# Tokens loaded ahead of the weights in the first modulation, and the last expert's rows added by a product

## The reference, cut to what matters

```python
# the first thing computed: the modulation of layer 0, from the vectors c and c_ctx
m_lat = adaln(c, w_mod[0], b_mod[0])          # silu(c) @ w_mod[0] + b_mod[0]; 1024 x 9216 weights
m_ctx = adaln(c_ctx[None], w_mod[0], b_mod[0])
# the last thing computed: each token goes to its two best experts of one group
yb  = (silu(xb @ w_gate[e]) * (xb @ w_up[e])) @ w_down[e]     # xb: up to 128 tokens of expert e
out = x + gate_1 * y_of_first_choice + gate_2 * y_of_second_choice
```

## Time and profile before

| | us |
|---|---|
| median of three executions | 3731.35 |
| lowest, highest | 3731.34, 3735.18 |
| the profiled execution's own time | 3733.24 |
| its span in the profile | 3731.5 |

### The profile page before, as it was taken

How to read it: one execution, slowest core, us unless ns; L and a number is a source line. 1 busy time by engine, 2 the same in 40 slices (tenths; PEclk the granted TensorE clock), 3 DMA queues, 4 the chain that set the end, 5 groups by cost and what they waited for, 6 DMA issues and landing times. The chain is left out here.

```text
span 3731.5 us, 44636 instructions
## 1 busy us (share of the span) xinstructions
PE 3499.3 (94%) x17456; PEld 2872.2 (77%) x17456; DVE 2191.0 (59%) x2933; ACT 1510.1 (40%) x1696; POOL 437.9 (12%) x321
## 2 busy tenths in 40 slices
PE   7999999888999999999989999798998998999996
PEld 5888888655888888888658888777876866888885
DVE  6635446548744466557886333552235337999996
ACT  4112111547422242223445222434444235777774
POOL 2000000200110011001112000200000012334441
PEclk9999999899999999999999999999998998999998
DMA  6333323210334325444112322131222326999996
GB/s 241 116 99 102 112 89 101 65 57 1 100 127 146 119 86 191 151 155 145 58 44 68 102 91 90 52 129 57 84 85 74 96 88 245 356 354 354 361 367 240
DMA packets 315224, 522.35 MB, mean 140 GB/s; under 512 B 18500, under 2 KB 274545, under 8 KB 289200
## 3 DMA queue, kind: packets, MB, share of 16 engines
q1 hardware_dynamic: 304016, 507.06, 39.5%
q0 software_dynamic: 11040, 12.91, 1.0%
HBM read 519.91 MB, written 25.17 MB: 146 GB/s over the span
## 5 line engine op out<-in xcount | busy, mean ns | idle before, releaser
L536 PE MATMUL banks<-operand_hi,trunk_weights_hi 128*128 128x512 f32 (+1 forms) x1568 | 568.4, 363 | 36.0 <-DVE operand_lo L1093 10.9
L536 PE MATMUL banks<-operand_lo,trunk_weights_hi 128*128 128x512 f32 (+1 forms) x1568 | 559.3, 357 | 0.0
L536 PE MATMUL banks<-operand_hi,trunk_weights_lo 128*128 128x512 f32 (+1 forms) x1568 | 559.2, 357 | 0.0
L536 PEld LDWEIGHTS banks<-operand_hi,trunk_weights_hi 128*128 128x128 f32 x1568 | 300.1, 191 | 84.0 <-issue 33.4
L536 PEld LDWEIGHTS banks<-operand_lo,trunk_weights_hi 128*128 128x128 f32 x1568 | 300.4, 192 | 41.3 <-issue 0.5
L536 PEld LDWEIGHTS banks<-operand_hi,trunk_weights_lo 128*128 128x128 f32 x1568 | 299.9, 191 | 41.5
L4172 DVE TENSOR_TENSOR ex_w_lo<-weight_ring,ex_w_hi 128x2048 fp32r<-128x2048 f32 x128 | 288.9, 2291 | 41.7 <-ACT ex_w_hi L4107 41.7
L1320 DVE TENSOR_TENSOR trunk_weights_lo<-weight_ring,trunk_weights_hi 128x2048 fp32r<-128x2048 f32 x90 | 206.6, 2296 | 177.1 <-ACT trunk_weights_hi L1275 177.1
L1275 ACT ACTIVATE trunk_weights_hi<-weight_ring 128x2048 fp32r<-128x2048 f32 x90 | 171.7, 1908 | 216.8 <-PE banks L536 216.3
L4107 ACT ACTIVATE ex_w_hi<-weight_ring 128x2048 fp32r<-128x2048 f32 x128 | 241.8, 1914 | 22.4 <-PE banks L4022 22.4
L536 PE MATMUL banks<-trunk_hidden_hi,trunk_weights_hi 128*128 128x512 f32 (+1 forms) x672 | 233.4, 347 | 4.4 <-DVE X L1822 1.9
(11 more groups left out here) (597 smaller groups left out, 7381.4 us busy)
## 6 DMA issues: line engine op xcount, KB each, us to landing
weight_ring<-ffn_w SPq DMA_DIRECT2D x120, 1024.0 KB, 5.2
weight_ring<-w_mod SPq DMA_DIRECT2D x72, 1024.0 KB, 5.1
weight_ring<-w_gate SPq DMA_DIRECT2D x64, 1024.0 KB, 6.1
weight_ring<-w_up SPq DMA_DIRECT2D x64, 1024.0 KB, 7.2
room<-w_down SPq DMA_DIRECT2D x64, 1024.0 KB, 7.2
weight_ring<-w_in SPq DMA_DIRECT2D x26, 1024.0 KB, 5.2
weight_ring<-ffn_w SPq DMA_DIRECT2D x16, 768.0 KB, 4.8
weight_ring<-o_w_pw SPq DMA_DIRECT2D x8, 1024.0 KB, 5.4
```

Source lines behind the costliest of these rows:

```text
L536: ins = pe.matmul(bank[:, at:at + width], w, x[:, at:at + width], start=start and n == 0, stop=stop and n == len(passes) - 1)
```

## The change

Opening:

- The tokens are the first large loads, as three of 1 MB with a semaphore each. Chunks 0 to 3 follow without a wait.
- All 48 transposes and 12 copies come before the first product, through the half banks 4, 5 and 7 instead of 0, 1, 2, 3 and 7.
- Each chunk is split and multiplied in two halves of 1024 columns, each with its own semaphore step: `w_hi`, `w_lo`, and four matmuls.
- The reload of a slot waits for the second half of its chunk.

End of the kernel:

- Routing also computes `last_gates`, the gate of each token towards the last slot column that runs, zero where it isn't there: four VectorE instructions.
- GpSimd, after the first two gathers, clears half of `YS`, copies the last slot column's ids, fills `hot` with 0 to 511, and scatters the zeros to the rows of the last column. It waits for these zeros before the second expert's scatter.
- The last expert's result is no longer scattered. ScalarE alone copies it to `YS`. VectorE makes `hot`, which is 1 where slot and token meet, and eight f32 matmuls of 512 columns multiply it with `YS`.
- The block `combine` is gone. In the experts' own block SP waits for the last weights' split and for GpSimd's word that all other scatters have landed, loads the chosen rows into the ring's four slots and stores the results. VectorE adds the chosen rows for all four tiles, then the product with `last_gates`, in eight halves of 512 columns.

```diff
@@ opening, SP
-            W.issue(sp, SLOTS)
-            W.used[0] = lambda i, r: (s_lo, r + 1)
-            W.issue(sp, SLOTS + 2)
-            sp.dma_start(rows[:, 0:ST, :], a["x"][0].rearrange("(t p) d -> p t d", p=P)).then_inc(s_x, 16)
-            sp.dma_start(rows[:, ST:, :], a["ctx"][0].rearrange("(t p) d -> p t d", p=P)).then_inc(s_x, 16)
-            W.ahead(sp, lambda i, r: (s_lo, r + 1))
+            for i, src in enumerate((a["x"][0][0:2 * P], a["x"][0][2 * P:], a["ctx"][0])):
+                sp.dma_start(rows[:, 2 * i:2 * i + 2, :], src.rearrange("(t p) d -> p t d", p=P)).then_inc(s_x[i], 16)
+            W.ahead(sp, lambda i, r: (s_lo, 2 * r + 2))
@@ opening, TensorE
+                for piece in range(2):
+                    pe.wait_ge(s_lo, 2 * n + piece + 1)
+                    for part, w in enumerate((w_hi, w_lo)):
+                        for q in range(2 * piece, 2 * piece + 2):
...
+            for j in range(2 * NT):
+                turn_tokens(j)
             pe.wait_ge(s_clo, 1)
@@ opening, ScalarE (VectorE alike, with its subtraction)
-                if n >= 2:
-                    act.wait_ge(s_done, n - 1)
-                act.activation(w_hi[:, n % 2, :], raw, ACT.Copy).then_inc(s_hi, 1)
+                for at in (0, 1024):
+                    if n >= 2:
+                        act.wait_ge(s_done, 2 * n - 3 + at // 1024)
+                    act.activation(w_hi[:, n % 2, at:at + 1024], raw[:, at:at + 1024], ACT.Copy).then_inc(s_hi, 1)
@@ routing, VectorE
+            link(dve.tensor_scalar(in_last[:], blk[:], cmax[:], -1.0, ALU.subtract, ALU.is_equal))
+            link(dve.tensor_tensor(in_last[:], in_last[:], hot[:, :, :, EXPERTS - 1].rearrange("p c t -> p (c t)"), ALU.mult))
+            link(dve.tensor_tensor(in_last[:], in_last[:], gates[:].rearrange("p c t -> p (c t)"), ALU.mult))
+            link(dve.tensor_tensor(last_gates[:], in_last[:, 0:ST], in_last[:, ST:], ALU.add))
@@ experts, SP
+            sp.wait_ge(s_lo, nth(n, 1, UP[1]))
+            sp.wait_ge(s_landed, 1)
+            for t in range(ST):
+                sp.dma_start(taken(t), chosen[:, :, t, :]).then_inc(s_y[t], 16)
+            for t in range(ST):
+                sp.wait_ge(s_sum, 2 * t + 2)
+                sp.dma_start(rows[:, t, :], XR[:, t, :]).then_inc(s_store, 16)
+            sp.wait_ge(s_store, 16 * ST)
@@ experts, GpSimd
             gather(0, 1)
+            pool.memset(YS[:, 1, :], 0.0).then_inc(s_clear, 1)
+            pool.tensor_copy(id_now[1][:], ids[:, span(n * 2 + 1, 1)]).then_inc(s_clear, 1)
+            pool.iota(hot, pattern=[[1, S]], base=0, channel_multiplier=0, allow_small_or_imprecise_dtypes=True).then_inc(s_lane, 1)
+            pool.wait_ge(s_clear, 2)
+            pool.indirect_dma_start(out=k.expert_out, out_offset=bass.IndirectOffsetOnAxis(ap=id_now[1][:, 0:1], axis=0),
+                                    in_=YS[:, 1, :], in_offset=None, bounds_check=2 * S - 1, oob_is_err=False).then_inc(s_zero, 16)
...
             scatter(n, 0)
-            scatter(n, 1)
-            for u in range(2):
-                pool.wait_ge(s_ys[u], n * 16 + 16)
+            pool.wait_ge(s_ys[0], n * 16 + 16)
+            pool.wait_ge(s_ys[1], n * 16)
+            pool.sem_inc(s_landed, 1)
@@ experts, TensorE
+            pe.wait_ge(s_hot, 1)
+            for t in range(ST):
+                for half in range(2):
...
+                    pe.matmul(OWN(t)[:, at], hot[:, t * P:(t + 1) * P], YS[:, 1, at], start=True, stop=True).then_inc(s_own, 1)
@@ experts, VectorE
-            rows_out(n, 2)
...
+            dve.tensor_scalar(hot, hot, token_last[:], None, ALU.is_equal).then_inc(s_hot, 1)
...
+                    dve.scalar_tensor_tensor(XR[:, t, :], taken(t)[:, c, :], gates[:, c, t:t + 1], XR[:, t, :], ALU.mult, ALU.add).then_inc(done, 1)
+            for t in range(ST):
+                dve.wait_ge(s_2, t + 1)
+                for half in range(2):
...
+                    dve.scalar_tensor_tensor(XR[:, t, at], OWN(t)[:, at], last_gates[:, t:t + 1], XR[:, t, at], ALU.mult, ALU.add).then_inc(s_sum, 1)
```

More of the change, by code:

```diff
@@ L356, in load_and_modulate @@
         sem = lambda n: k.sem(f"ld_{n}")
-        s_con, s_first, s_vec, s_x, s_zero, s_clear, s_vt, s_vc, s_silu, s_chi, s_clo = (
-            sem("consts"), sem("first_vectors"), sem("vectors"), sem("tokens"), sem("vector_zeros"), sem("cleared"), sem("vectors_turned"),
+        s_x = [sem(f"tokens{i}") for i in range(NT // 2)]
+        s_con, s_first, s_vec, s_zero, s_clear, s_vt, s_vc, s_silu, s_chi, s_clo = (
+            sem("consts"), sem("first_vectors"), sem("vectors"), sem("vector_zeros"), sem("cleared"), sem("vectors_turned"),
             sem("vectors_copied"), sem("silu"), sem("cond_hi"), sem("cond_lo"))
@@ L420, in product @@
             def product(n):
[L421 to L427, removed]
+                for piece in range(2):
+                    pe.wait_ge(s_lo, 2 * n + piece + 1)
+                    for part, w in enumerate((w_hi, w_lo)):
+                        for q in range(2 * piece, 2 * piece + 2):
+                            kk, r = (n, q) if n < KD else (2 * (n - KD) + q // 2, 4 + q % 2)
+                            ins = pe.matmul(half(r), cond4[:, kk, :], w[:, n % 2, 512 * q:512 * q + 512],
+                                            start=kk == 0 and part == 0, stop=kk == KD - 1 and part == 1)
+                    ins.then_inc(s_done, 1)
             pe.wait_ge(s_con, 16)
@@ L509, in _ @@
                 if c == KD:
[L510 removed]
+                    dve.wait_ge(s_done, 2 * KD)
                     for r in (1, 3):
@@ L3632, in mixture @@
         k.raw_landed = [k.sem(f"ex_raw_landed{c}") for c in range(CHUNKS)]
-        project_and_route(k, MX, XR, XG, gates, pairs, ids, tokens)
-        experts(k, XR, XG, pairs, ids, tokens)
-        combine(k, XR, gates, out)
+        project_and_route(k, MX, XR, XG, gates, last_gates, pairs, ids, tokens)
+        experts(k, XR, XG, pairs, ids, tokens, gates, last_gates, out)
 CHUNKS = 6
@@ L3931, in _, with experts @@
                 pool.tensor_tensor(squares[:, 0, :], squares[:, 0, :], squares[:, m, :], ALU.add).then_inc(s_sum, 1)
-def experts(k, XR, XG, pairs, ids, tokens):
+def experts(k, XR, XG, pairs, ids, tokens, gates, last_gates, out):
     nc = k.nc
@@ L3953, in experts @@
         s_free = [sem(f"rows_free{i}") for i in range(2)]
+        s_y = [sem(f"chosen{t}") for t in range(ST)]
+        s_landed = sem("rows_landed")
+        s_clear, s_zero, s_lane, s_token, s_hot, s_1, s_2, s_own, s_sum, s_store = (
+            sem("rows_cleared"), sem("zeros_scattered"), sem("lanes"), sem("last_token"), sem("last_hot"), sem("first_choice"),
+            sem("second_choice"), sem("last_rows"), sem("sums"), sem("stored"))
+        token_last = sb("token_last", [P, 1])
+        hot = k.x_sum[:, 0:S]
+        chosen = k.expert_out.rearrange("(c t p) d -> p c t d", c=2, p=P)
+        taken = lambda t: k.weights.ring[:, t, :].rearrange("p (c d) -> p c d", c=2)
+        rows = out[0].rearrange("(t p) d -> p t d", p=P)
+        OWN = lambda t: k.PS[(0, 1, 3, 2)[t]]
         block = st.enter_context(nc.Block())
@@ L4228, in _ @@
             chunk_lo(n, 2, DOWN[1])
[L4229 to L4253 removed]
+            dve.tensor_copy(token_last[:], tokens[:, span(n * 2 + 1, 1)]).then_inc(s_token, 1)
+            dve.wait_ge(s_lane, 1)
+            dve.wait_ge(s_token, 1)
+            dve.tensor_scalar(hot, hot, token_last[:], None, ALU.is_equal).then_inc(s_hot, 1)
             for t in range(ST):
```

93 lines of the change are left out of this document (37 added, 56 removed).

## The result

The changed kernel takes **3711.12 us** (median of 4 runs, 3707.02 to 3713.69), against 3731.35 us before (median of 4 in the same session, 3729.94 to 3735.18): ratio 0.9943, 95% interval 0.9926 to 0.996, so 20.2 us faster. The profiled execution has a span of 3709.9 us and an own time of 3712.35, against 3731.5 and 3733.24 before. The forecast was 3711.5. The span is 21.6 us shorter, and the table shows where.

A forecast was written before the change was run, and what follows sets the result against it. TensorE is busy 94% of the 3731.5 us span, so an edit pays only where it stands still. Opening -5.9, routing +0.8, experts' start 0 and tail -14.8 sum to -19.9: 3731.35 becomes 3711.5 us, range 3707 to 3720.

The forecast's parts named there:

- Opening, -5.9 predicted: First modulation stage: tokens loaded first and chunks in halves end it at 56.2 instead of 62.13 us, 5.9 us saved.
- end near 17: Opening: the context's four halves, transposed at half clock, finish near 17 us, 2 us after the first weight chunk is in.
- Splitting adds 24 instructions and 24 waits: Opening: cost of halving chunks on VectorE and ScalarE, included in 1.22 and 1.04 us per half.
- Routing, 0.8: End of routing: four more VectorE instructions in the chain behind the count, 0.8 us lost, bounds 0.6 to 1.0.
- Experts' start, 0: Start of the experts: GpSimd's clearing and zero scatter, some 3.0 us, cost nothing; bounds 0 to 1.3 us lost.
- Tail, -14.8: End of the kernel: last expert's rows added from SBUF and an earlier reload, end at 3716.7, 14.8 us saved.
- The Trainium skill's 358 GB/s: Opening: the page's HBM rate per core gives 2.93 us a load and a stage end at 58.2; forecast kept 2.65.
- One slow product is hidden behind the landings: Opening: a single product at 1.2 GHz after the transposes costs nothing; only a low clock that stays does.
- Rival A: Tail: the wait released by the landed scatter takes the full 8.96 us, delaying the reload; 3715.8 us, chance 0.18.
- B: Opening: TensorE stays at half clock, so the stage ends 18.5 us after the forecast; 3730.0 us, chance 0.05.
- C: Experts' loop: loads come to lead it, each of 31 periods growing by 1 us; 3742.5 us, chance 0.03.
- D: Opening: the stage ends where it did and only the tail gains; 3717.4 us, chance 0.11.

## Why the prediction was right, and where it was not

The time, the signs and the shares of both parts came out. That the median fell within 0.4 us of the forecast is luck: the span shrank by 21.6 us where the sum had 19.9, the opening and the tail gave 1.6 and 1.05 more than forecast, the experts' loop 0.5, the stretch between took 1.4 of that back, and the four runs spread over 7 us. Point by point:

- **Opening, -5.9 predicted, -7.5 measured.** The landings were right: chunk 11 by 44.2, its use at 44.80; 2.65 us a load, 2.62 measured. The error is the term "end near 17", the context's halves at half clock. Their sixteen transposes took 2.00 us, not 3.6, at a granted clock of 1.00 from 13 to 16 us; the last copy ended near 16, chunk 0 was taken as it landed, and VectorE began at 17.07 instead of 18.1. Its 24 halves took 28.86 us (19.61, 2.36 and 6.89), not 29.3. Its last half was done at 48.64, not 50, and TensorE's queue behind it, which the prediction had in the right order, ended as much earlier. One sign was missed: ScalarE waited 1.75 us for chunk 8, where no wait over 1 us was forecast.
- **The reading of the opening was incomplete.** That "token transposes, their copies and the column products are threaded between the last four chunks, and each engine waits for the next" is true but was one limit of two. Taken away alone it gives nothing, since the loop through two tiles takes its place (62.84); with halves it is worth 4.45 us (59.08 to 54.63). The halves were priced as pure overhead ("Splitting adds 24 instructions and 24 waits"). The experiments show that the whole gain hangs on them or on a third tile: with whole chunks through two tiles the new order saves nothing. The sum came out because it costed the kernel with both edits, and VectorE and the DMA do limit that one. For the order alone, the same reasoning led me to expect an end at 54.6 to 55.5; that the change had both edits in it was luck for the forecast.
- **Routing, 0.8: 0.87.** Four links, as priced. **Experts' start, 0:** nothing, and nothing when doubled.
- **Tail, -14.8: -15.85.** The reload came 3.36 us after the scatter, against 3.5 predicted. From the last subtraction: to the first addition 0.59 us instead of 0.84; eight additions 10.15 instead of 10.3; eight small ones 5.35 (0.67 each) instead of 5.9 (0.73); the store 3.1 as predicted. The small additions are the mis-sized term: the 0.73 came from a 0.75, and eight in a row take 0.67 each. TensorE's pairs came every 7.11 / 8 = 0.89 us, against 0.9.
- **The Trainium skill's 358 GB/s** (DMA: Bandwidth & Descriptors, Specifications), which would have put the stage's end at 58.2: the window shows 421 GB/s, and the measurement decides.
- **Product 0 and the clock.** In the profile of the result the first two matmuls of product 0 took 0.70 us at a granted 1.00, after 48 transposes and 3.14 us of standing still. Most other executions differ. In seven of the ten profiles with the tokens first, the granted clock fell to 0.5 just before product 0 or within 0.4 us of its start. The two that stood still for only 2.7 us kept 2.4 GHz, the three that stood still for 4.7 to 5.0 us did not, and of the five with 3.13 to 3.19 us one did. The Trainium skill's rule on transposes (TensorE: Matmul & The Clock Gate, Part 4: PE-mode transpose), by which product 0 would start at 1.2 GHz, fits those seven and not the other three. Standing still explains as much: after 4.88 us of it behind products, with no transposes, the clock of the kernel before fell too, and no run has a pause of some 3.1 us without transposes. The prediction's "One slow product is hidden behind the landings" held: with the low clock at product 0 the opening ended at 54.53 and 54.79, without it at 54.63 and 54.70. Product 0 in the second profile of the changed kernel, then in that of the kernel with the columns earlier:

```profile
18.34 0.86 PE L425 MATMUL banks<-ada_w_hi,ada_cond 128*128 128x512 f32 x2 [3.13 <-DVE ada_w_lo L494]
```

```profile
18.46 1.19 PE L425 MATMUL banks<-ada_w_hi,ada_cond 128*128 128x512 f32 x2 [3.19 <-DVE ada_w_lo L494]
```

- **Rival A** (late reload) is out by 3.36 us; what spoke for it was real, since the block boundary did hold 5.65 us. The prediction's argument against A, that "neither GpSimd nor a boundary as such is slow", was wrong of this boundary. The forecast did not rest on it, since its own sum took 3.2 us "since the block's end is gone". **B** (a clock that stays down) did not happen in the profile of the result. Late in the opening it did in two others, for 7 us (between 40 and 50 us, with the zeros twice) and for 14 us (from 47 us on, three tiles), at a price of 3 and 7 us. The same openings had no such fall in other executions. **C** is out: the loop took 604.45 us against 604.91. **D** is out: the opening alone ended at 54.70.

## What to carry to other kernels

Before you price an earlier load, walk once round the tiles: the sum of the stages that a tile passes, over the number of tiles, is the least time per chunk. Where it is above the landing time, here 3.25 against 2.49 us, the order of loads was worth nothing until the chunk was halved or a tile was added. Two edits that save little each were worth three times their sum together (7.5 us against 3.05 - 0.7). A tail behind the last item of a loop can be cut twice: let the reload wait in the loop's own block (5.8 us here), and keep the last item out of the round trip through DRAM (10 us).

## What the hardware showed that was not expected

- TensorE's granted clock differs between executions of one kernel at the same place: 63.33 against 56.33 us for the end of one opening, 3038.78 against 3031.73 us for one stretch. The fall in the three-tile kernel was not foretold by what the engine did just before: from 40 to 45 us it was busy 2.61 us in one execution and 2.12 in the other, and it was the busier one that fell. What decides the level in an execution stayed open.
- Where the low clock falls decides its price. At product 0, where the landings set the pace, it cost the changed opening nothing; between 40 and 60 us, where TensorE's queue ends the block, it cost 3 and 7 us. Where none fell between 40 and 54 us, the changed opening's end repeats within 0.3 us (54.53, 54.63, 54.70, 54.79). For a change of a few us in one stage this is a better measure than a whole time that varies by 7.
- A block boundary behind an indirect scatter cost 5.65 us, where another boundary costs VectorE 0.63. What fills it was not tried.
